# Last stage of a hybrid attention and MoE layer: the expert-row adds of six blocks on GpSimd, stores from the sync engine, one output buffer a block

## The chip, the cores and the metric

The kernel runs on one core of one Trainium2 chip. The metric is the device time of one execution in microseconds; for the kernel before it is the median of three runs. Smaller is better. A profile of one further execution gives the rows below.

## The reference, cut to what matters

The reference is one layer: 16 meta tokens are put ahead of 1024 frames of 1024 channels; RMSNorm, a combined input projection, two attention branches (latent attention, and sparse attention over 256 selected keys), gates, an output projection and a residual; then RMSNorm and a mixture of experts in which each token goes to two experts. The change touches only the end, which in the reference reads:

```python
out = jnp.zeros((N + 1, D), ys.dtype).at[slot_tok].add(ys * slot_w[:, None].astype(ys.dtype))
...
h = h + ffn.reshape(B, L, D_MODEL)
return rmsnorm(h, norm_final_g)[:, N_META:]
```

For each of the 1024 frames the two weighted expert rows are added, the sum is added to the residual `h`, and the row is normalised: divided by the root of its mean square plus 1e-6, times a gain for each channel. All of it is float32.

## The kernel before

The kernel is written for each engine by hand: every stage is a block in which each engine has its own list of instructions, and semaphores hold them together. An engine runs its list in order; a wait stops everything behind it on that engine. The stages are the norm and the projections, the attention branches, the gated output projection, the router tables, the loop over 32 experts (`experts`), a stage for experts with more than 128 rows (`overflow`), and the last stage, the function `final`. The experts leave their weighted rows in DRAM, in `ys_d`: 2048 rows of 4 KB, the first expert row of token t at t and the second at 1024 + t. The last stage starts when all of them are written.

`final` works on 8 blocks of 128 tokens (`NB` = 8, `P` = 128, `D` = 1024), one partition for each token. For block b:

- SyncE loads the two expert rows into `ya[b]` and `yb[b]` (tiles `fa` and `fb` in the trace), 512 KB each. All 16 loads, and the broadcast of the final gain into `gf`, are issued without any wait, since every block has buffers of its own. They go through the sync engine's queue.
- VectorE adds `yb[b]` to `ya[b]` (L2342), then adds that to the residual `h1[:, b, :]` (L2344, tile `h`).
- ScalarE squares the row and sums it (L2316, tile `fsq`, sum in `ss`).
- GpSimd makes the mean plus epsilon (L2325, `var`), then the power -0.5 (L2327, `rstd`), both on 128x1.
- VectorE multiplies the row by `rstd` and the gain into an output buffer (`finish`, L2337, tile `fo`), one block behind its adds: its order is fa(0), h(0), fa(1), h(1), fo(0), fa(2), h(2), fo(1), and so on up to fa(7), h(7), fo(6), fo(7).
- ScalarE issues the store of `fo` behind the square of the next block (L2319). There are four output buffers, so `finish(b)` for b from 4 on waits for the store of block b - 4.

Of the kernel before, what the change touches and what calls it, by code (L numbers as in the profile page):

```python
# [14 lines left out]
ALU = mybir.AluOpType  # L15
ACT = mybir.ActivationFunctionType
AX = mybir.AxisListType
F32 = mybir.dt.float32
# [4 lines left out]
P = 128  # L23
D = 1024
# [4 lines left out]
NB = T // P  # L29
# [1856 lines left out]
def experts(nc, a, at, sem, block, ps, flat, con, h1, nhalf, tabs, xn2_d, ys_d, out, R_H, R_K, ss, var, rstd,  # L1886
# [26 lines left out]
    with block() as blk:  # L1913
# [185 lines left out]
        def _(dve):  # L2099
# [72 lines left out]
            with dve.Fori(0, (NE - 4) // 4) as r:  # L2172
# [6 lines left out]
    overflow(nc, a, at, sem, block, ps, ident, xs, ye, xsT, sg, hm, hmT, tk, dk, wk, wts,  # L2179
             tok_i, dst_i, slot_w, ov_e, xn2_d, ys_d)  # L2180
    final(nc, a, at, sem, block, h1, nhalf, ys_d, out, R_K, R_H, ss, var, rstd)


# [104 lines left out]
def final(nc, a, at, sem, block, h1, nhalf, ys_d, out, R_K, R_H, ss, var, rstd):  # L2288

    ya = [at(f"fa{b}", [P, D], F32, R_K + 8192 * b) for b in range(NB)]  # L2290
    yb = [at(f"fb{b}", [P, D], F32, R_K + 8192 * b + 4096) for b in range(NB)]
    gf = at("gfin", [P, D], F32, R_K + 65536)
    sq = at("fsq", [P, D], F32, R_K + 69632)
    fo = [at(f"fo{k}", [P, D], F32, R_K + 73728 + 4096 * k) for k in range(4)]
    s_g, s_a1, s_a2, s_sq, s_v, s_r, s_o = map(sem, ["f_g", "f_a1", "f_a2", "f_sq", "f_v", "f_r", "f_o"])
    s_ls = [sem(f"f_l{b}") for b in range(NB)]
    s_sts = [sem(f"f_st{k}") for k in range(4)]
    with block() as blk:  # L2298
        @blk.sync
        def _(sp):  # L2300
            for b in range(NB):
                for k, t in enumerate((ya, yb)):
                    sp.dma_start(t[b][:, :], ys_d[T * k + P * b:T * k + P * (b + 1), :]).then_inc(s_ls[b], 16)  # L2303
                if b == 0:
                    sp.dma_start(gf[:, :], a["norm_final_g"].unsqueeze(0).to_broadcast([P, D])).then_inc(s_g, 16)  # L2305
            for k in range(4):
                sp.wait_ge(s_sts[k], 16 * NB // 4)

        @blk.scalar
        def _(act):  # L2310
            for b in range(NB + 1):
                if b < NB:
                    act.wait_ge(s_a2, b + 1)
                    if b:
                        act.wait_ge(s_sq, b)
                    act.activation(sq[:, :], h1[:, b, :], ACT.Square, accum_out=ss[:, b:b + 1]).then_inc(s_sq, 1)  # L2316
                if b:
                    act.wait_ge(s_o, b)
                    act.dma_start(out[0, P * (b - 1):P * b, :], fo[(b - 1) % 4][:, :]).then_inc(s_sts[(b - 1) % 4], 16)  # L2319

        @blk.gpsimd
        def _(pool):
            for b in range(NB):
                pool.wait_ge(s_sq, b + 1)
                pool.tensor_scalar(var[:, b:b + 1], ss[:, b:b + 1], 1.0 / D, EPS, ALU.mult, ALU.add).then_inc(s_v, 1)  # L2325
                pool.wait_ge(s_v, b + 1)
                pool.tensor_tensor(rstd[:, b:b + 1], var[:, b:b + 1], nhalf[:, b:b + 1], ALU.pow).then_inc(s_r, 1)  # L2327

        @blk.vector
        def _(dve):  # L2330
            def finish(b):
                dve.wait_ge(s_r, b + 1)
                if b == 0:
                    dve.wait_ge(s_g, 16)
                if b >= 4:
                    dve.wait_ge(s_sts[b % 4], 16 * (b // 4))
                dve.scalar_tensor_tensor(fo[b % 4][:, :], h1[:, b, :], rstd[:, b:b + 1], gf[:, :], ALU.mult,  # L2337
                                         ALU.mult).then_inc(s_o, 1)

            for b in range(NB):  # L2340
                dve.wait_ge(s_ls[b], 32)
                dve.tensor_tensor(ya[b][:, :], ya[b][:, :], yb[b][:, :], ALU.add).then_inc(s_a1, 1)  # L2342
                dve.wait_ge(s_a1, b + 1)
                dve.tensor_tensor(h1[:, b, :], h1[:, b, :], ya[b][:, :], ALU.add).then_inc(s_a2, 1)  # L2344
                if b:
                    finish(b - 1)
            finish(NB - 1)
# [21 lines left out]
```

## Time and profile before

| what | value |
|---|---|
| median of 3 runs | 1633.92 us (1629.78 to 1636.15) |
| the profiled execution: its own time | 1635.34 us |
| its span in the trace | 1633.4 us |
| first DMA issue of the last stage | 1591.14 us from the span's start |
| busy over the whole span: PE, DVE, ACT, POOL | 1434.7, 1052.9, 650.6, 405.3 us |

The last stage is the last 42.3 us of the span, 2.6% of it. PE does nothing there, so the shares of the whole span say nothing about it; what counts is the order of the small instructions on DVE (VectorE), ACT (ScalarE), POOL (GpSimd) and of the DMAs. Every time below is in us from the start of the span, unless it is marked ns. An instruction's row in the trace begins when its engine takes it up; where it is held up after that, its own duration in the row is longer.

### The profile page before, as it was taken

The numbers are of one execution on the slowest core, as the hardware profiler recorded it, in microseconds if no ns is written. First come the engines' busy times: TensorE is split into PE (matmuls) and PEld (weight loads), VectorE is DVE, ScalarE is ACT, GpSimd is POOL, SyncE is SP. The second block draws the span as 40 slices with busy tenths as digits, with TensorE's granted clock in tenths as the row PEclk, the third lists the DMA queues.
The fourth block names the chain that finished last, engine by engine and source line by source line (L and its number), as shares of the span: only waits on it lengthen the run. The fifth ranks groups of instructions, "written<-read, shape, count | busy, mean of one in ns | idle before, by whom it ended". The sixth has DMA issues, their size and how long they took to land. (4 is left out here: it accounts for less than half of the span.)

```text
span 1633.4 us, 21404 instructions
## 1 busy us (share of the span) xinstructions
PE 1434.7 (88%) x7182; PEld 1108.7 (68%) x7191; DVE 1052.9 (64%) x2047; ACT 650.6 (40%) x1129; POOL 405.3 (25%) x406
## 2 busy tenths in 40 slices
PE   6996899999999898988889888999945999999960
PEld 3465688889895457777667666889944777777730
DVE  4158999999922466666676665443254777777737
ACT  3157212121211236666666654021103666666622
POOL 1000322221211105454434411410002233333213
PEclk9998899999999999999999998999966999999985
DMA  7450122332231000302323204423154899999808
GB/s 195 51 87 14 58 81 87 103 97 91 73 117 42 1 0 1 72 1 66 75 60 82 66 1 161 157 87 104 65 219 182 321 357 357 356 367 376 328 31 319
DMA packets 86604, 216.82 MB, mean 133 GB/s; under 512 B 23720, under 2 KB 46792, under 8 KB 74232
## 3 DMA queue, kind: packets, MB, share of 16 engines
q1 hardware_dynamic: 76152, 194.72, 36.4%
q0 software_dynamic: 9216, 16.80, 2.8%
q10 hardware_dynamic: 1152, 4.19, 0.6%
q8 instruction: 51, 0.84, 0.2%
q14 instruction: 33, 0.27, 0.1%
HBM read 187.75 MB, written 44.70 MB: 142 GB/s over the span
## 5 line engine op out<-in xcount | busy, mean ns | idle before, releaser
L1193 DVE TENSOR_TENSOR pL<-ps,pH 128x512 fp32r<-128x512 f32 (+3 forms) x224 | 127.0, 574 | 114.4 <-ACT pH L1130 113.6
L457 DVE TENSOR_SCALAR_CACHE_REDUCE mask<-score,cand 128x272 bf16<-128x272 f32 (+6 forms) x224 | 185.5, 892 | 5.0 <-DVE cand L476 4.9
L2102 DVE TENSOR_TENSOR w_rest<-wgu,w_lead 128x1024 fp32r<-128x1024 f32 x128 | 156.0, 1223 | 45.0 <-ACT w_lead L2049 43.8
L542 PE MATMUL ps<-hHi,g_lead 128*128 128x512 f32 (+2 forms) x416 | 158.6, 381 | 16.2 <-DVE hLo L582 16.2
L543 PE MATMUL ps<-hLo,g_lead 128*128 128x512 f32 (+2 forms) x416 | 158.8, 382 | 0.0
L544 PE MATMUL ps<-hHi,g_rest 128*128 128x512 f32 (+2 forms) x416 | 158.0, 380 | 0.0
L2049 ACT CAST w_lead<-wgu 128x1024 fp32r<-128x1024 f32 x128 | 134.4, 1055 | 37.9 <-PE ps L1995 37.9
L1130 ACT CAST pH<-ps 128x512 fp32r<-128x512 f32 (+3 forms) x224 | 107.7, 488 | 71.5 <-PE ps L1078 70.5
L1993 PE MATMUL ps<-w_lead,x_lead 128*128 128x512 f32 x256 | 114.2, 446 | 6.0 <-DVE w_rest L2102 6.0
L577 POOL TENSOR_TENSOR g_rest<-g_raw,g_lead 128x2048 fp32r<-128x2048 f32 x13 | 61.7, 4745 | 227.8 <-ACT g_lead L551 227.8
L2015 PE MATMUL ps<-wd,hmT 128*128 128x512 f32 x256 | 115.3, 593 | 1.6 <-DVE hmT L2125 1.0
L1995 PE MATMUL ps<-w_lead,x_rest 128*128 128x512 f32 x256 | 101.8, 397 | 0.0
L542 PEld LDWEIGHTS ps<-hHi,g_lead 128*128 128x128 f32 x416 | 79.0, 190 | 32.9 <-issue 11.2
L1994 PE MATMUL ps<-w_rest,x_lead 128*128 128x512 f32 x256 | 100.9, 394 | 0.0
L1094 PE MATMUL ps<-pH,VS 128*128 128x512 f32 (+3 forms) x224 | 98.5, 440 | 0.2
L544 PEld LDWEIGHTS ps<-hHi,g_rest 128*128 128x128 f32 x416 | 79.1, 190 | 13.9
L543 PEld LDWEIGHTS ps<-hLo,g_lead 128*128 128x128 f32 x416 | 78.9, 190 | 14.0
L1955 POOL DMA_INDIRECT ys_d<-ye,dk x32 | 32.5, 1015 | 213.7 <-DVE ye L2137 213.7
L1095 PE MATMUL ps<-pL,VS 128*128 128x512 f32 (+3 forms) x224 | 81.4, 363 | 0.0
L563 ACT ACTIVATE stage<-ps 128x512 f32<-128x512 f32 x32 | 19.2, 598 | 151.9 <-PE ps L544 151.9
L2015 PEld LDWEIGHTS ps<-wd,hmT 128*128 128x128 f32 x256 | 46.2, 190 | 47.8 <-issue 47.8
L356 PE MATMUL ps<-hT,wslot 128*128 128x512 f32 (+2 forms) x176 | 72.1, 573 | 2.3 <-DMA wslot<-in_w_in 2.3
(332 smaller groups left out, 3453.1 us busy)
## 6 DMA issues: line engine op xcount, KB each, us to landing
wgu<-in_w_exp_gate SPq DMA_DIRECT2D x32, 1024.0 KB
wgu<-in_w_exp_up SPq DMA_DIRECT2D x32, 1024.0 KB
wd<-in_w_exp_down SPq DMA_DIRECT2D x32, 1024.0 KB
g_raw<-in_w_in SPq DMA_DIRECT2D x14, 1024.0 KB, 5.5
gates_d<-stage SPq DMA_DIRECT2D x32, 256.0 KB, 2.0
gt<-gates_d SPq DMA_DIRECT2D x32, 256.0 KB, 3.2
rel_d<-relf SPq DMA_DIRECT2D x1, 4672.0 KB
KR<-kb_d SPq DMA_DIRECT2D x16, 260.0 KB, 6.0
```

The lines of the kernel that those rows point to most:

```text
L457: return dve.tensor_scalar(mask[:, OFF[i]:OFF[i + 1]], score[:, OFF[i]:OFF[i + 1]], thr, 0.0, op, ALU.add, accum_out=cnt[:, i:i + 1])
L542: pe.matmul(dst, x[0], y[0], start=(k == 0), stop=False)
L543: pe.matmul(dst, x[0], y[1], start=False, stop=False)
L544: mm = pe.matmul(dst, x[1], y[0], start=False, stop=(k == KT - 1))
L1130: act.copy(pH[n % RING][:, lo:512], bank_of(k)[:, lo:512]).then_inc(s_ld, 1)
L1193: dve.tensor_tensor(pL[n % RING][:, lo:512], bank_of(k)[:, lo:512], pH[n % RING][:, lo:512].bitcast(F32), ALU.subtract).then_inc(s_rs, 1)
L1993: pe.matmul(dst, xl[:, k, :], wl, start=(k == 0), stop=False)
L1994: pe.matmul(dst, xl[:, k, :], wr, start=False, stop=False)
L1995: mm = pe.matmul(dst, xr[:, k, :], wl, start=False, stop=(k == KT - 1))
L2015: mm = pe.matmul(ps[:, 5 + half, :], hmT[u % 2][:, k, :], wd[u][:, k, 512 * half:512 * (half + 1)], start=(k == 0), stop=(k == 1))
L2049: act.copy(w_lead[part][:, :, :, :], wgu[u][:, :, 2 * part:2 * part + 2, :]).then_inc(S["m_wl"], 1)
L2102: dve.tensor_tensor(w_rest[u][:, :, 2 * part:2 * part + 2, :], wgu[u][:, :, 2 * part:2 * part + 2, :], w_lead[part][:, :, :, :].bitcast(F3 ...
```

## The change

In `final`, the add of the two expert rows for blocks 1 to 6 is made by GpSimd, one block ahead of its `var` and `rstd`: its list becomes add(b + 1), var(b), rstd(b). VectorE keeps that add for blocks 0 and 7 and waits for GpSimd's in between. The stores are issued by SyncE behind all the loads, each once the loads of a block four later (or of the last) have landed and `fo` of its block is written; ScalarE issues none. There are eight output buffers in place of four, so `finish` waits for no store.

```diff
--- before.py
+++ after.py
@@ -2291,10 +2291,11 @@
     yb = [at(f"fb{b}", [P, D], F32, R_K + 8192 * b + 4096) for b in range(NB)]
     gf = at("gfin", [P, D], F32, R_K + 65536)
     sq = at("fsq", [P, D], F32, R_K + 69632)
-    fo = [at(f"fo{k}", [P, D], F32, R_K + 73728 + 4096 * k) for k in range(4)]
-    s_g, s_a1, s_a2, s_sq, s_v, s_r, s_o = map(sem, ["f_g", "f_a1", "f_a2", "f_sq", "f_v", "f_r", "f_o"])
+    fo = [at(f"fo{b}", [P, D], F32, R_K + 73728 + 4096 * b) for b in range(NB)]
+    s_g, s_ad, s_ap, s_h, s_sq, s_v, s_r, s_o, s_st = map(
+        sem, ["f_g", "f_ad", "f_ap", "f_h", "f_sq", "f_v", "f_r", "f_o", "f_st"])
     s_ls = [sem(f"f_l{b}") for b in range(NB)]
-    s_sts = [sem(f"f_st{k}") for k in range(4)]
+    on_pool = range(1, NB - 1)
     with block() as blk:
         @blk.sync
         def _(sp):
@@ -2303,24 +2304,26 @@
                     sp.dma_start(t[b][:, :], ys_d[T * k + P * b:T * k + P * (b + 1), :]).then_inc(s_ls[b], 16)
                 if b == 0:
                     sp.dma_start(gf[:, :], a["norm_final_g"].unsqueeze(0).to_broadcast([P, D])).then_inc(s_g, 16)
-            for k in range(4):
-                sp.wait_ge(s_sts[k], 16 * NB // 4)
+            for b in range(NB):
+                sp.wait_ge(s_ls[min(b + 4, NB - 1)], 32)
+                sp.wait_ge(s_o, b + 1)
+                sp.dma_start(out[0, P * b:P * (b + 1), :], fo[b][:, :]).then_inc(s_st, 16)
+            sp.wait_ge(s_st, 16 * NB)
 
         @blk.scalar
         def _(act):
-            for b in range(NB + 1):
-                if b < NB:
-                    act.wait_ge(s_a2, b + 1)
-                    if b:
-                        act.wait_ge(s_sq, b)
-                    act.activation(sq[:, :], h1[:, b, :], ACT.Square, accum_out=ss[:, b:b + 1]).then_inc(s_sq, 1)
+            for b in range(NB):
+                act.wait_ge(s_h, b + 1)
                 if b:
-                    act.wait_ge(s_o, b)
-                    act.dma_start(out[0, P * (b - 1):P * b, :], fo[(b - 1) % 4][:, :]).then_inc(s_sts[(b - 1) % 4], 16)
+                    act.wait_ge(s_sq, b)
+                act.activation(sq[:, :], h1[:, b, :], ACT.Square, accum_out=ss[:, b:b + 1]).then_inc(s_sq, 1)
 
         @blk.gpsimd
         def _(pool):
             for b in range(NB):
+                if b + 1 in on_pool:
+                    pool.wait_ge(s_ls[b + 1], 32)
+                    pool.tensor_tensor(ya[b + 1][:, :], ya[b + 1][:, :], yb[b + 1][:, :], ALU.add).then_inc(s_ap, 1)
                 pool.wait_ge(s_sq, b + 1)
                 pool.tensor_scalar(var[:, b:b + 1], ss[:, b:b + 1], 1.0 / D, EPS, ALU.mult, ALU.add).then_inc(s_v, 1)
                 pool.wait_ge(s_v, b + 1)
@@ -2329,19 +2332,22 @@
         @blk.vector
         def _(dve):
             def finish(b):
-                dve.wait_ge(s_r, b + 1)
                 if b == 0:
                     dve.wait_ge(s_g, 16)
-                if b >= 4:
-                    dve.wait_ge(s_sts[b % 4], 16 * (b // 4))
-                dve.scalar_tensor_tensor(fo[b % 4][:, :], h1[:, b, :], rstd[:, b:b + 1], gf[:, :], ALU.mult,
+                dve.wait_ge(s_r, b + 1)
+                dve.scalar_tensor_tensor(fo[b][:, :], h1[:, b, :], rstd[:, b:b + 1], gf[:, :], ALU.mult,
                                          ALU.mult).then_inc(s_o, 1)
 
+            added = 0
             for b in range(NB):
-                dve.wait_ge(s_ls[b], 32)
-                dve.tensor_tensor(ya[b][:, :], ya[b][:, :], yb[b][:, :], ALU.add).then_inc(s_a1, 1)
-                dve.wait_ge(s_a1, b + 1)
-                dve.tensor_tensor(h1[:, b, :], h1[:, b, :], ya[b][:, :], ALU.add).then_inc(s_a2, 1)
+                if b in on_pool:
+                    dve.wait_ge(s_ap, b - on_pool[0] + 1)
+                else:
+                    dve.wait_ge(s_ls[b], 32)
+                    added += 1
+                    dve.tensor_tensor(ya[b][:, :], ya[b][:, :], yb[b][:, :], ALU.add).then_inc(s_ad, 1)
+                    dve.wait_ge(s_ad, added)
+                dve.tensor_tensor(h1[:, b, :], h1[:, b, :], ya[b][:, :], ALU.add).then_inc(s_h, 1)
                 if b:
                     finish(b - 1)
             finish(NB - 1)
```

VectorE, from the start of the stage. The numbers behind tile names tell buffers apart: `fa_14653` is `ya[1]`, `fb_14661` is `yb[1]`, `fo_14670` is the first output buffer. The kernel before:

```order
L2342 TENSOR_TENSOR fa_14652<-fa_14652,fb_14660 128x1024
L2344 TENSOR_TENSOR h_10538<-h_10538,fa_14652 128x1024
L2342 TENSOR_TENSOR fa_14653<-fa_14653,fb_14661 128x1024
L2344 TENSOR_TENSOR h_10538<-h_10538,fa_14653 128x1024
L2337 SCALAR_TENSOR_TENSOR fo_14670<-h_10538,rstd,gfin 128x1024
L2342 TENSOR_TENSOR fa_14654<-fa_14654,fb_14662 128x1024
L2344 TENSOR_TENSOR h_10538<-h_10538,fa_14654 128x1024
L2337 SCALAR_TENSOR_TENSOR fo_14671<-h_10538,rstd,gfin 128x1024
```

The same place in the changed kernel:

```order
L2348 TENSOR_TENSOR fa_14652<-fa_14652,fb_14660 128x1024
L2350 TENSOR_TENSOR h_10538<-h_10538,fa_14652 128x1024
L2350 TENSOR_TENSOR h_10538<-h_10538,fa_14653 128x1024
L2338 SCALAR_TENSOR_TENSOR fo_14670<-h_10538,rstd,gfin 128x1024
L2350 TENSOR_TENSOR h_10538<-h_10538,fa_14654 128x1024
L2338 SCALAR_TENSOR_TENSOR fo_14671<-h_10538,rstd,gfin 128x1024
```

The adds of `fa` are gone from VectorE for blocks 1 to 6; the order of what is left is the same.

GpSimd, from its first instruction of the stage, in the changed kernel (before, the stage's list held only the pairs of `var` and `rstd`):

```order
L2326 TENSOR_TENSOR fa_14653<-fa_14653,fb_14661 128x1024
L2328 TENSOR_SCALAR var<-ss 128x1
L2330 TENSOR_TENSOR rstd<-var,nhalf 128x1
L2326 TENSOR_TENSOR fa_14654<-fa_14654,fb_14662 128x1024
L2328 TENSOR_SCALAR var<-ss 128x1
L2330 TENSOR_TENSOR rstd<-var,nhalf 128x1
```

The add of block 1 now stands ahead of the `var` and `rstd` of block 0, the add of block 2 ahead of those of block 1, up to block 6.

## Rows read from the trace of the kernel before

**Rows 1.** The chain that ended last: start, duration, what.

```profile
1593.04 8.18 DMA fb<-ys_d
...
1601.24 1.24 DVE fa L2342
...
1628.98 1.28 DVE fo L2337
```

**Rows 2.** Timeline, first blocks: start, duration, engine, line, operation, idle before.

```profile
1599.65 0.19 POOL L2325 TENSOR_SCALAR var<-ss 128x1 f32<-128x1 f32 x1 [18.35 <-ACT fsq L2316]
...
1599.92 0.57 POOL L2327 TENSOR_TENSOR rstd<-var,nhalf 128x1 f32<-128x1 f32 x1
...
1600.85 1.06 SPq L2303 DMA_DIRECT2D fb<-ys_d  x1
...
1604.84 1.22 DVE L2342 TENSOR_TENSOR fa<-fa,fb 128x1024 f32<-128x1024 f32 x1
...
1604.99 1.11 POOL L2325 TENSOR_SCALAR var<-ss 128x1 f32<-128x1 f32 x1 [4.49 <-ACT fsq L2316]
1606.09 1.23 DVE L2344 TENSOR_TENSOR h<-h,fa 128x1024 f32<-128x1024 f32 x1
1606.18 1.53 POOL L2327 TENSOR_TENSOR rstd<-var,nhalf 128x1 f32<-128x1 f32 x1
...
1607.75 1.28 DVE L2337 SCALAR_TENSOR_TENSOR fo<-h,rstd,gfin 128x1024 f32<-128x1024 f32 x1 [0.44 <-POOL rstd L2327]
...
1608.58 0.50 POOL L2325 TENSOR_SCALAR var<-ss 128x1 f32<-128x1 f32 x1 [0.86 <-ACT fsq L2316]
1608.95 1.22 DVE L2342 TENSOR_TENSOR fa<-fa,fb 128x1024 f32<-128x1024 f32 x1
...
1609.17 1.41 POOL L2327 TENSOR_TENSOR rstd<-var,nhalf 128x1 f32<-128x1 f32 x1
```

**Rows 3.** Timeline, last blocks.

```profile
1616.67 1.22 DVE L2342 TENSOR_TENSOR fa<-fa,fb 128x1024 f32<-128x1024 f32 x1
...
1623.18 1.28 DVE L2337 SCALAR_TENSOR_TENSOR fo<-h,rstd,gfin 128x1024 f32<-128x1024 f32 x1 [0.44 <-POOL rstd L2327]
...
1625.63 1.23 DVE L2344 TENSOR_TENSOR h<-h,fa 128x1024 f32<-128x1024 f32 x1
```

**Rows 4.** Windows of the stage: engines' busy us (count), clock, DMA share, GB/s.

```profile
1610.00:1615.00 5.00, 0.00 (x0) 0.00 (x0) 4.93 (x5) 1.15 (x2) 2.79 (x3) 0.50 1.03 420
...
1620.00:1625.00 5.00, 0.00 (x0) 0.00 (x0) 4.53 (x5) 1.48 (x4) 3.56 (x4) 0.50 0.29 119
```

**Rows 5.** GpSimd groups of the whole span: operation, shapes, count, busy us, mean ns.

```profile
L1259 POOL TENSOR_TENSOR KL<-KTa,KH 96x1040 fp32r<-96x1040 f32 x7 | 17.0, 2422 | 0.6
L1240 POOL TENSOR_TENSOR q_rest<-QTa,q_lead 96x1024 fp32r<-96x1024 f32 x7 | 16.6, 2377 | 0.6
```

**Rows 6.** Timeline of GpSimd and of VectorE, 1019 to 1024 us.

```profile
1019.58 1.29 POOL L1584 TENSOR_TENSOR yT<-ytmp 128x512 f32<-128x512 f32 x1 [7.02 <-DVE ytmp L1517]
1022.14 2.13 POOL L1584 TENSOR_TENSOR yT<-ytmp 128x512 f32<-128x512 f32 x1 [1.28 <-DVE ytmp L1517]
...
1021.91 1.22 DVE L1499 TENSOR_TENSOR wb_rest<-wbr,wb_lead 128x1024 fp32r<-128x1024 f32 x1
```

**Rows 7.** Line L582, both engines: duration ns min/median/max, first and last start.

```profile
L582 POOL TENSOR_TENSOR hLo<-hT,hHi x4: 2572/3394/3401, 160.3 to 169.5; 128x1040 fp32r<-128x1040 f32 x4
L582 DVE TENSOR_TENSOR hLo<-hT,hHi x4: 3426/3430/3442, 160.5 to 170.6; 128x1040 fp32r<-128x1040 f32 x4
```

**Rows 8.** GpSimd's first two of these in its timeline.

```profile
160.28 2.57 POOL L582 TENSOR_TENSOR hLo<-hT,hHi 128x1040 fp32r<-128x1040 f32 x1 [135.64 <-ACT hHi L555]
...
162.82 3.40 POOL L582 TENSOR_TENSOR hLo<-hT,hHi 128x1040 fp32r<-128x1040 f32 x1
```

**Rows 9.** The stage's stores: ns of an issue on ScalarE's queue, min/median/max.

```profile
L2319 ACTq DMA_DIRECT2D out<-fo x8: 338/338/395, 1605.0 to 1630.3; - x8
```

## The prediction

> **What bounds the stage now.** I read the chain that ended last first, because the change lies in the last 42 us and only what ends last there can move the time. The chain waits for the loads of block 1 until 1601.22 [rows 1]; from there it never leaves the loop VectorE, ScalarE, GpSimd, VectorE. The timeline of the stage shows what that loop costs: VectorE's add of block 2 starts at 1604.84 and that of block 5 at 1616.67 [rows 2, 3], three blocks in 11.83 us, so 3.94 a block early on. Its own work in a block is fa 1.22, h 1.23 and fo 1.28, which overlap by some hundredths. So VectorE is nearly full, as the windows say too (4.5 to 4.9 us busy in 5) [rows 4]. The DMA engines are at 1.03 of their time from 1610 to 1615 and at 0.29 from 1620 to 1625 [rows 4], so the transfers are nearly through while the loop still has 10 us to go. The last fo begins at 1628.98 and ends at 1630.26 [rows 1]; the last store is some 3.1 us more, to the end of the span at 1633.4.
>
> On its face, then, the change takes a third of the work off the engine that bounds. The second thing to read is what GpSimd's tiny instructions do beside VectorE. Alone, var takes 0.19 and rstd 0.57 [rows 2]. Beside VectorE, var takes 1.11 (1604.99 to 1606.10, and VectorE's fa ends at 1606.06) and rstd 1.53 (1606.18 to 1607.71, and h ends at 1607.32). The next rstd ends 0.41 after VectorE's fa. So a GpSimd instruction that reads SBUF is held until VectorE's instruction with two SBUF inputs ends, and then finishes 0.04 (var) or 0.40 (rstd) later. It holds beside fo as well: var of 1608.58 ends at 1609.08, and fo at 1609.03 [rows 2]. It also slips in there between two VectorE instructions that follow each other.
>
> **What a GpSimd add costs, alone and beside VectorE.** The trace has no GpSimd add of this very shape, but near ones: 2.38 us for 1024 columns, 2.42 for 1040 [rows 5], and 1.29 for 512 columns of plain float32 on 128 partitions [rows 6], which is the same rate. I take 2.38. Held up by VectorE, the 512-column add took 2.13: VectorE's instruction ended at 1023.13, the add at 1024.27, 1.14 later, so it has 0.15 of its 1.29 behind it while it waits [rows 6]. A held add of 1024 columns then ends 2.23 after VectorE's.
>
> The other direction is at 160 to 174 us, where both engines made two-input subtractions of 1040 columns, four each. GpSimd's took 3.39 to 3.40 and VectorE's 3.43 [rows 7], where one alone is 2.42 and about 1.25. GpSimd's first two end at 162.85 and 166.22 [rows 8], 3.37 apart: 2.27 of GpSimd and 1.10 of VectorE, strictly one after the other. So VectorE is held as fully as GpSimd, and comes out 1.10 after the add ends; I take 1.09 for 1024 columns.
>
> The Trainium skill has this as a rule ("SBUF — State Buffer", section "Who interferes with whom"): a VectorE instruction with two SBUF inputs and a GpSimd instruction that reads SBUF exclude each other, and the second one blocks until the first is done. The trace agrees in both directions, with the overlap of about 0.15 that the rows give. By the rule taken literally, with full durations in turn, the result is the heavy rival below; by the rows it is the sum that follows.
>
> **The change, part by part.** *The adds.* All of VectorE's instructions here (fa, h, fo) have two SBUF inputs, and so has GpSimd's add. What was 1.2 us of VectorE becomes 2.2 to 2.4 us in which VectorE can't work either. Start: block 1 lands at 1601.21 as before (the loads ahead of it are the same); GpSimd adds from 1601.24 to 1603.62. Which of two goes first afterwards, the next add or the waiting fo, the trace doesn't tell (they become ready within some 0.05 us), so I work out both.
>
> (A) The add goes first. From the end of one add: held fo(b-1) 1.09, h(b+1) directly behind it 1.23 - 0.08 = 1.15 (fo to fa starts are 1.20 apart at a duration of 1.28 [rows 2]), var slips in, rstd 0.40 after h, the next add 2.38: 5.02 a block. The first round has no fo: 0.03 + 1.23 + 0.40 + 2.38 = 4.04. The add of block 6 ends at 1603.62 + 4.04 + 4 x 5.02 = 1627.74. Then fo(4) 1.09, h(6) 1.15, rstd(5) 0.40, 0.02 to start fo(5); from the start of fo(5) to the end of h(7) as before (1623.18 to 1626.86 [rows 3]: 3.68); and from there to the end of fo(7) as before (to 1630.26: 3.40). Last fo ends at 1637.48: 7.2 later.
>
> (B) fo goes first. A round is 0.03 + 1.23 (h), 0.40 (rstd), 0.02 + 1.28 (fo), 2.23 (held add): 5.19. Block 6's add ends at 1603.62 + 5 x 5.19 = 1629.57, and 1.26 + 0.40 + 0.02 + 3.68 + 3.40 = 8.76 more gives 1638.33: 8.1 later.
>
> The two bound the orders; I take the middle, +7.6.
>
> *var and rstd behind the add.* rstd(0) is late by the whole add of block 1; that is in the rounds above. Behind it on GpSimd waits only the next add.
>
> *Loads.* They are ahead all the time: at the 420 GB/s of [rows 4] a block's 1.05 MB takes 2.5, so block b lands at about 1601.2 + 2.5 (b - 1) with no store between, block 6 at 1613.7, and its add is not due before 1625.
>
> *Stores.* The last store alone is on the path. Its issue is 0.34 on ScalarE's queue [rows 9]; one of SyncE's issues took 1.06 at 1600.85, with many transfers queued [rows 2], and at the end there are next to none. I take +0.1, between 0 and 0.7. The stores that queue behind loads wait for nobody, with eight buffers. All loads are issued by 1601.9 [rows 2], so no store stands ahead of one. In the kernel before fo(5) waits for rstd, not for its buffer's store [rows 3], so four more buffers free nothing. ScalarE loses eight issues in its idle time: nothing.
>
> *Sum:* +7.7 on the profiled execution's own 1635.34, so 1643.0 for a profiled one; the profiled run is 1.4 above the median 1633.92, and against the median it gives 1641.6.
>
> **Rivals.**
> - *No exclusion for this add* (the GpSimd add reads beside VectorE). GpSimd would need 2.38 + 0.19 + 0.57 and 0.15 of gaps, 3.3 a block; block 6's add at 1603.62 + 16.5 = 1620.1, the last fo at 1620.1 + 1.26 + 0.02 + 3.68 + 3.40 = 1628.5, 1.8 earlier: 1632.1. For it speaks only that GpSimd is idle enough; against it the eight instructions of line L582 [rows 7]. It decides if the adds take 2.4 in the stage while VectorE's rows stay at 1.2. Even with no cost on GpSimd at all, block 7 lands at 1616.2 and needs fa and h 2.49 and the tail 3.40: 1622.1, a gain of 8.2. A gain over 0.5% (8.2 us) is therefore out of reach.
> - *Heavy handing over.* Each of the five instructions of a round costs its full own duration in turn: 1.28 + 1.23 + 0.19 + 0.57 + 2.38 and 0.15 of gaps, 5.8. Block 6's add at 1603.62 + 29.0 = 1632.6, the last fo 8.8 later at 1641.4: +11.1, so 1645.0. For it: VectorE now hands over three times in a round. Against it: each handing over in the rows was cheaper than that.
> - *VectorE keeps the port for two instructions in a row and GpSimd waits for both,* or the other way round. In (A) and (B) VectorE never has more than two to give; one more wait of 0.4 a block gives +9.7, so 1643.6.
>
> **How the numbers follow.** The serial sum between 7.2 and 8.1 (1641 to 1642 against the median): 0.75. Heavy handing over or the extra wait: 0.17. No exclusion: 0.05; the rest is something unseen. The three runs of before spread by 6 us, so a median of a few runs is good to about 2 us; a difference can be told from none at about 0.5%, which is 8.2 us. My sum ends right under that bound, 0.47%. Below it fall a bit over half of the serial case and the no-exclusion case, above it the rest and the heavy cases: same 0.50, slower 0.46, faster 0.04. The range 1636.8 to 1645.8 leaves out no exclusion and the far end of the heavy case.
>
> **What would show it.** In the profile after: GpSimd's adds of about 4.5 to 4.7 where held by fo and h, or 2.4 where VectorE waits; VectorE's h or fo beside them with rows of 2.5 to 3.5 or idle time put down to GpSimd's `fa`; about 5.0 to 5.2 us from one h to the next for blocks 2 to 6, against 3.9 before; the last fo near 1638; DMA share falling to near zero well before the end; and in the chain that ended last, GpSimd's add with 10 us or more in place of VectorE's. The prediction is wrong if h to h is under 4 (then there is no exclusion) or over 5.5 (then handing over costs more), or if the last store lands more than 4 us after the last fo.

## The result, and the profile after

Over all runs the changed kernel takes 1638.96 us (median of 15, 1635.75 to 1643.21) and the kernel before 1631.02 us (median of 15, 1626.76 to 1636.19). The ratio is 1.0047, 95% interval 1.0034 to 1.0060: 7.7 us slower, 5.5 to 9.8. The forecast was +7.7 us and 1641.6 us in a range of 1636.8 to 1645.8. It was added to the median of three runs of the kernel before, 1633.92.

The two profiled spans, 1633.4 and 1636.1 us, are only 2.7 apart. The reason lies ahead of the change: the last stage begins at 1591.14 in the one and at 1587.17 in the other, and in the eight experiments between 1582.25 and 1590.87, though nothing ahead of it differs. So the stage itself is compared, from its first DMA issue: 42.26 us before (to 1633.4), 48.93 after (to 1636.1). Within it the cleanest stretch is from the moment block 1 is ready (the start of its add) to the end of the last fo: 29.02 us before, 36.12 after, a difference of 7.10. Below, this is called the stretch, and a round is the time from the start of one h to the start of the next.

The chain that ended last, in the changed kernel: start, duration, what. One round in the middle and the tail:

```profile
1589.12 7.73 DMA fb<-ys_d
...
1596.92 2.33 POOL fa L2326
...
1606.17 2.31 POOL fa L2326
1608.48 0.08 issue
1608.57 1.06 POOL var L2328
1609.62 0.07 issue
1609.70 1.41 POOL rstd L2330
1611.11 2.31 POOL fa L2326
...
1625.95 1.28 DVE fo L2338
1627.23 1.15 DVE fa L2348
```

From block 1 to block 6 the chain now goes through GpSimd alone: add, var, rstd, add. Of the 4.94 us of a round only 2.31 is the add; the 1.06 and 1.41 belong to two instructions that need 0.19 and 0.55 to 0.57 alone. Where that time goes is seen in the timeline of the same round (compare [rows 2]):

```profile
1606.14 2.34 POOL L2326 TENSOR_TENSOR fa<-fa,fb 128x1024 f32<-128x1024 f32 x1
1606.20 3.36 DVE L2338 SCALAR_TENSOR_TENSOR fo<-h,rstd,gfin 128x1024 f32<-128x1024 f32 x1 [0.44 <-POOL rstd L2330]
...
1608.57 1.05 POOL L2328 TENSOR_SCALAR var<-ss 128x1 f32<-128x1 f32 x1
1609.49 1.21 DVE L2350 TENSOR_TENSOR h<-h,fa 128x1024 f32<-128x1024 f32 x1
1609.70 1.41 POOL L2330 TENSOR_TENSOR rstd<-var,nhalf 128x1 f32<-128x1 f32 x1
...
1611.08 2.34 POOL L2326 TENSOR_TENSOR fa<-fa,fb 128x1024 f32<-128x1024 f32 x1
1611.14 3.36 DVE L2338 SCALAR_TENSOR_TENSOR fo<-h,rstd,gfin 128x1024 f32<-128x1024 f32 x1 [0.44 <-POOL rstd L2330]
```

VectorE's fo starts 0.06 us behind GpSimd's add and stays in its row for 3.36 us, 1.08 of them after the add has ended (1608.48 to 1609.56). Then var is done 0.06 after fo, h runs until 1610.70, and rstd is done 0.41 after h. Apart from a tenth or two at each change from one engine to the other, no two of the five do their work side by side. The six adds read alike, none of them held. Of the eight fo, the five beside an add take 3.28 to 3.36 us, and the three with no add beside them 1.28. The views of the two lines (duration in ns, min/median/max):

```profile
L2326 POOL TENSOR_TENSOR fa<-fa,fb x6: 2333/2337/2342, 1596.9 to 1621.0; 128x1024 f32<-128x1024 f32 x6
```

```profile
L2338 DVE SCALAR_TENSOR_TENSOR fo<-h,rstd,gfin x8: 1278/3318/3364, 1601.3 to 1631.8; 128x1024 f32<-128x1024 f32 x8
```

A window shows how "busy" misleads here, against the same window in [rows 4]: both engines look nearly full, and the DMA engines are idle three quarters of the time.

```profile
1620.00:1625.00 5.00, 0.00 (x0) 0.00 (x0) 4.56 (x3) 1.15 (x2) 4.83 (x4) 0.50 0.26 105
```

VectorE is shown busy for 4.56 of 5 us with three instructions in the window; in the kernel before it was 4.53 us with five.

### The profile page after: what moved, and what is told of

Its sections match the earlier page's. It is cut to its first block and busy times, and to the rows that moved or that the text cites. A ratio compares the mean times of both kernels' runs of the same rounds, so it can differ in the third digit from the quotient of the medians.

```text
span 1636.1 us, 21406 instructions
## 1 busy us (share of the span) xinstructions
PE 1432.5 (88%) x7182; PEld 1107.0 (68%) x7191; DVE 1056.0 (65%) x2041; ACT 650.8 (40%) x1129; POOL 422.1 (26%) x412
## 5 line engine op out<-in xcount | busy, mean ns | idle before, releaser
L1213 POOL TENSOR_TENSOR otok<-otmp,rec 128x256 f32<-128x256 f32 x32 | 19.7, 614 | 214.7 <-DVE otmp L1200 214.7
```

## The experiments

All were compared with the kernel before on the same chip. The stretch is read from the profiled execution, one for each kernel.

| kernel | stretch, us | against 29.02 | ratio to before, 95% interval |
|---|---|---|---|
| the change | 36.12 | +7.10 | 1.0047 (1.0034 to 1.0060) |
| adds_only | 36.10 | +7.08 | 1.0031 (1.0017 to 1.0045) |
| stores_only | 29.01 | -0.01 | 0.9998 (0.9986 to 1.0011) |
| gain_psum | 32.69 | +3.67 | 1.0023 (1.0011 to 1.0034) |
| both_psum | 26.77 | -2.25 | 0.9989 (0.9976 to 1.0002) |
| three_adds | 32.02 | +3.00 | 1.0018 (1.0009 to 1.0028) |
| no_adds_psum | 27.39 | -1.63 | 0.9989 (0.9976 to 1.0002) |
| three_adds_psum | 25.65 | -3.37 | 0.9984 (0.9972 to 0.9996) |
| three_late_psum | 25.54 | -3.48 | 0.9990 (0.9978 to 1.0001) |

The theory is that VectorE's instructions with two SBUF inputs and GpSimd's that read SBUF exclude each other, so that an add moved to GpSimd takes 2.2 us from VectorE in place of 1.2. The rivals are the stores' new place, a loss from GpSimd's latency or list whatever it reads, and a cost that is paid once and not for each add.

### Half of the change each: adds_only and stores_only

adds_only takes the changed kernel and puts the stores back as they were, with four output buffers (cut to the store itself):

```diff
-                sp.dma_start(out[0, P * b:P * (b + 1), :], fo[b][:, :]).then_inc(s_st, 16)
...
+                    act.dma_start(out[0, P * (b - 1):P * b, :], fo[(b - 1) % 4][:, :]).then_inc(s_sts[(b - 1) % 4], 16)
```

> The six adds go to GpSimd as in the change; the stores stay on ScalarE's queue with four output buffers, as before. If the cost is the port that VectorE and GpSimd exclude each other from, the whole loss is here: a round of 4.94 us between the starts of h for blocks 2 to 6, as in the changed kernel, the last fo some 36.1 us after block 1 is ready (29.0 before), and a ratio to before of 1.004 to 1.005. If the loss (or a part of it) came from the stores behind the loads on SyncE's queue, the round is shorter and the ratio nearer 1.

stores_only keeps the stores and puts the adds back on VectorE:

```diff
-    on_pool = range(1, NB - 1)
+    on_pool = []
```

> SyncE issues the stores behind the loads, with eight output buffers; all adds stay on VectorE. If the port is the cause: a round of 3.86 us as before, 29.0 us from block 1 ready to the last fo, 3.1 us from there to the end, ratio 1.000 (within 0.15%). If the stores' place costs or gains: more or less than 3.1 us at the end, or waits of fo.

adds_only repeats the changed kernel's stretch to 0.02 us, stores_only that of before to 0.01. From the end of the last fo to the end of the span it is 3.14 us before, 3.06 in the changed kernel, 3.10 and 3.11 in these two. The ratio of adds_only, 1.0031, is lower than the expected 1.004 to 1.005, but its interval holds the 1.0043 that 7.1 us would make. So the loss is in the adds, and the stores' queue and the four more buffers cost or bring nothing that these runs can show.

### Taking the exclusion away and leaving the adds: gain_psum and both_psum

gain_psum reads the final gain from PSUM (`flat` is the PSUM tile), where ScalarE copies it once (1.02 us, while it waits for loads); `finish(0)` waits for that copy in place of the load:

```diff
+    gp = flat[:, 0:D]
...
+            act.wait_ge(s_g, 16)
+            act.copy(gp, gf[:, :]).then_inc(s_gp, 1)
...
-                dve.scalar_tensor_tensor(fo[b][:, :], h1[:, b, :], rstd[:, b:b + 1], gf[:, :], ALU.mult,
+                dve.scalar_tensor_tensor(fo[b][:, :], h1[:, b, :], rstd[:, b:b + 1], gp, ALU.mult,
```

> The changed kernel, with the final gain copied once to PSUM by ScalarE, so that VectorE's fo has one SBUF input in place of two; everything else as in the changed kernel. If two SBUF inputs are what excludes GpSimd: fo falls from 3.36 us in its row to about 1.3 and lies beside the add of 2.33; a round is h 1.26, var 0.11 behind it, rstd 0.57, add 2.33, about 4.3 us in place of 4.94, and the stage some 3.5 us shorter than the changed kernel's (ratio to before about 1.002 to 1.003). If VectorE is held by a GpSimd instruction whatever it reads: fo stays at 3.3 and the round at 4.94, ratio 1.0047.

Timeline of gain_psum, one round:

```profile
1609.42 2.35 POOL L2330 TENSOR_TENSOR fa<-fa,fb 128x1024 f32<-128x1024 f32 x1
1609.49 1.28 DVE L2342 SCALAR_TENSOR_TENSOR fo<-h,rstd,ps 128x1024 f32<-128x1024 f32 x1 [0.71 <-POOL rstd L2334]
...
1611.80 1.22 DVE L2354 TENSOR_TENSOR h<-h,fa 128x1024 f32<-128x1024 f32 x1 [1.03 <-POOL fa L2330]
1611.85 1.22 POOL L2332 TENSOR_SCALAR var<-ss 128x1 f32<-128x1 f32 x1
...
1613.15 0.55 POOL L2334 TENSOR_TENSOR rstd<-var,nhalf 128x1 f32<-128x1 f32 x1
```

The same fo starts 0.07 us behind the same add, and takes 1.28 where it took 3.36. Nothing else was changed on VectorE or GpSimd, so it is the gain read from SBUF, fo's second input there, that let the add hold it. The round is 4.25 (h starts at 1607.55 and 1611.80), as worked out. What still has two SBUF inputs, h, still holds var: 1.22 in place of 0.19.

both_psum does the same for h. ScalarE copies each block's residual to PSUM ahead of its add, three slots in turn:

```diff
+                if b + 3 < NB:
+                    act.copy(hp(b + 3), h1[:, b + 3, :]).then_inc(s_hp, 1)
...
-                dve.tensor_tensor(h1[:, b, :], h1[:, b, :], ya[b][:, :], ALU.add).then_inc(s_h, 1)
+                dve.wait_ge(s_hp, b + 1)
+                dve.tensor_tensor(h1[:, b, :], hp(b), ya[b][:, :], ALU.add).then_inc(s_h, 1)
```

> As the one before, and ScalarE also copies each block of the residual to PSUM ahead of h's add (three slots in turn), so that neither h nor fo has two SBUF inputs. With the port theory nothing but the fa of blocks 0 and 7 excludes GpSimd any more: var 0.19, rstd 0.57, add 2.33 and gaps 0.2 to 0.3 make a round of about 3.3 us, bound by GpSimd; the last fo comes about 27 us after block 1 is ready, 2 us sooner than before; ratio about 0.999. If ScalarE's extra copies (about 1.1 us a block beside the square of 1.25) or slower reads of PSUM bind, the round is longer than 3.3; if the exclusion has another cause, it stays above 4.9.

Timeline of both_psum, one round:

```profile
1610.09 1.23 DVE L2364 TENSOR_TENSOR h<-ps,fa 128x1024 f32<-128x1024 f32 x1 [0.82 <-POOL fa L2339]
1610.14 0.19 POOL L2341 TENSOR_SCALAR var<-ss 128x1 f32<-128x1 f32 x1
1610.42 0.55 POOL L2343 TENSOR_TENSOR rstd<-var,nhalf 128x1 f32<-128x1 f32 x1
1610.93 2.35 POOL L2339 TENSOR_TENSOR fa<-fa,fb 128x1024 f32<-128x1024 f32 x1
1611.23 1.27 DVE L2351 SCALAR_TENSOR_TENSOR fo<-h,rstd,ps 128x1024 f32<-128x1024 f32 x1
```

Now every row of the round has the duration that it has alone, within 0.02 us, var 0.19 and rstd 0.55 among them, and the round is 3.23 us, GpSimd's own list from end to end. VectorE waits 0.82 for each add. The only long row left is a var of 1.10 us at 1622.28, beside VectorE's add of block 7, which still reads two tiles from SBUF. The kernel with the six adds, 7.10 us behind the kernel before with the exclusion, is 2.25 ahead of it without: this is the prediction's first rival, made true (its round was 3.3 us and its gain 1.8). How much of the 2.25 the moved adds bring is measured below. The ratio, 0.9989, can't be told from 1.

Here the Trainium skill ("SBUF — State Buffer", section "Who interferes with whom") says that a VectorE instruction with at most one SBUF input, outside the modes that use both ports, does not contend with GpSimd. The rows of both kernels agree (fo 1.28 beside the add in gain_psum, var 0.19 beside h in both_psum).

### Half the dose: three_adds

```diff
-    on_pool = range(1, NB - 1)
+    on_pool = [2, 4, 6]
```

> The changed kernel with GpSimd's adds for blocks 2, 4 and 6 only; VectorE makes the other five. All from SBUF. If each moved add costs the difference of the two engines' exclusive time (2.2 of GpSimd for 1.2 of VectorE), two blocks take about 8.7 us where before took 7.7 and the changed kernel 9.9; the last fo comes some 32 us after block 1 is ready (29.0 before, 36.1 changed), ratio about 1.002. If a cost of another kind (the first wait on GpSimd, the order on its list) made the loss, three adds cost as much as six, 36 us.

Timeline of three_adds, one moved add with what holds it and what it holds:

```profile
1610.08 1.41 POOL L2330 TENSOR_TENSOR rstd<-var,nhalf 128x1 f32<-128x1 f32 x1
1611.12 1.22 DVE L2350 TENSOR_TENSOR h<-h,fa 128x1024 f32<-128x1024 f32 x1
1611.46 3.08 POOL L2326 TENSOR_TENSOR fa<-fa,fb 128x1024 f32<-128x1024 f32 x1
1612.26 3.37 DVE L2338 SCALAR_TENSOR_TENSOR fo<-h,rstd,gfin 128x1024 f32<-128x1024 f32 x1
```

Three adds cost 3.00 us in the stretch, 1.00 for each, where six cost 7.10, 1.18 for each. Two blocks take 8.54 (h at 1607.01 and 1615.55), against 8.7 expected. Here both directions are seen at once: the add waits for h, which ends at 1612.34, and comes 2.20 later at 1614.54; fo waits for the add and comes 1.09 after it. A loss that is only paid once is excluded.

### Is it PSUM that gains? no_adds_psum

The kernel both_psum with `on_pool = []`: all adds on VectorE.

> No add on GpSimd; the gain and the residual are read from PSUM, so that h and fo have one SBUF input each; stores as in the changed kernel. With the port theory rstd is held by fa alone, the waits of 0.44 us in every second block go, and the round falls from 3.86 to about 3.6 us: the last fo 27.2 to 27.5 us after block 1 is ready, ratio 0.999. If PSUM inputs in themselves changed VectorE's pace, its rows of 1.22 to 1.28 would change; if they did nothing, 29.0.

```profile
1607.84 1.23 DVE L2364 TENSOR_TENSOR h<-ps,fa 128x1024 f32<-128x1024 f32 x1
1607.94 0.55 POOL L2343 TENSOR_TENSOR rstd<-var,nhalf 128x1 f32<-128x1 f32 x1
1608.98 1.27 DVE L2351 SCALAR_TENSOR_TENSOR fo<-h,rstd,ps 128x1024 f32<-128x1024 f32 x1
1610.17 1.22 DVE L2361 TENSOR_TENSOR fa<-fa,fb 128x1024 f32<-128x1024 f32 x1
```

VectorE's rows are as long as before (1.22 to 1.27), and the round is 3.58 in place of alternately 3.59 and 4.12: rstd, beside h, takes 0.55 and not 1.53 and is no longer late. The kernel before itself lost 1.6 us to the exclusion: three of its rounds had the wait of 0.44 that [rows 2, 3] show in front of fo, and each of them was 0.53 longer than the others. So PSUM alone brings 1.63 of both_psum's 2.25, and six adds on GpSimd only 0.6 more: with six, GpSimd's list of 3.23 us a round binds.

### Three adds without the exclusion: three_adds_psum and three_late_psum

three_adds_psum is both_psum with `on_pool = [3, 5, 7]`.

> Gain and residual from PSUM, GpSimd's adds for blocks 3, 5 and 7. Nothing but VectorE's own fa excludes GpSimd. VectorE is left with 21 instructions of about 1.2 us in place of 24; GpSimd's add, behind its rstd, comes about 0.6 us late in every second block. The last fo 25 to 26 us after block 1 is ready, 3 to 4 sooner than before; ratio 0.9975 to 0.9985. Rival: the loads, which need 15 us from block 1 to block 7, or GpSimd's latency bind, and it is no better than 27.

```profile
1606.20 1.22 DVE L2361 TENSOR_TENSOR fa<-fa,fb 128x1024 f32<-128x1024 f32 x1
1606.37 1.10 POOL L2341 TENSOR_SCALAR var<-ss 128x1 f32<-128x1 f32 x1 [1.62 <-ACT fsq L2330]
...
1607.55 0.55 POOL L2343 TENSOR_TENSOR rstd<-var,nhalf 128x1 f32<-128x1 f32 x1
1608.07 2.36 POOL L2339 TENSOR_TENSOR fa<-fa,fb 128x1024 f32<-128x1024 f32 x1
1608.59 1.27 DVE L2351 SCALAR_TENSOR_TENSOR fo<-h,rstd,ps 128x1024 f32<-128x1024 f32 x1
...
1610.45 1.23 DVE L2364 TENSOR_TENSOR h<-ps,fa 128x1024 f32<-128x1024 f32 x1 [0.59 <-POOL fa L2339]
```

25.65 us, 3.37 below before, and a ratio of 0.9984 whose interval (0.9972 to 0.9996) ends just below 1 and holds the 0.9979 that 3.37 us would make: of all versions, this is the only one whose timed runs show it ahead of the kernel before. The wait of 0.6 in front of h in every second block is the one that the expectation named. The rows above say more of it. The add stands behind var and rstd, and this var is held by VectorE's fa, the one kind of instruction with two SBUF inputs that is left: 1.10 us in place of 0.19. An estimate from these rows: with a var of 0.19 the add would end 0.9 sooner, and the wait of 0.6 would be gone. No run tests that.

three_late_psum adds one edit to it:

```diff
-                if b:
-                    finish(b - 1)
-            finish(NB - 1)
+                if b >= 2:
+                    finish(b - 2)
+            finish(NB - 2)
+            finish(NB - 1)
```

> As the one before, and VectorE's fo comes two blocks behind h in place of one, so that neither a late rstd nor the last square holds it. VectorE should run without a gap from block 3 on: 24 to 25 us from block 1 ready to the last fo, ratio 0.997. If it isn't below three_adds_psum by 0.5 us or more in that stretch, the latency of rstd was not what was left.

This was a miss. The stretch is 25.54, only 0.11 shorter. The last fo no longer waits 0.94 for its rstd, but h of block 3 now waits 1.31 in place of 0.60, since one fo less stands ahead of it and the add waits for its loads (0.59 on GpSimd). Outside the stretch 0.9 is lost again: the last stores are issued closer together, and the span ends 4.01 us after the last fo instead of 3.13. The ratios of the two versions can't be told apart. The later blocks still wait 0.6 for the add, so fo's wait for rstd was not what cost them that. What did is the add's place on GpSimd's list, behind a var that fa holds here too (1.10 us at 1610.20, beside fa at 1610.04):

```profile
1607.71 1.23 DVE L2364 TENSOR_TENSOR h<-ps,fa 128x1024 f32<-128x1024 f32 x1 [1.31 <-POOL fa L2339]
...
1614.29 1.22 DVE L2364 TENSOR_TENSOR h<-ps,fa 128x1024 f32<-128x1024 f32 x1 [0.59 <-POOL fa L2339]
```

Neither another order on that list (the add ahead of the var and rstd of two blocks back) nor an fa with one input in PSUM was tried, so how the 0.6 divides between the two stays open. That the last stores compete is read from one profile and not tested.

## Why the prediction was right

**What bounds.** Right: VectorE's list with its short waits for rstd. What the prediction did not say is that these waits were already the exclusion's; no_adds_psum put 1.63 us on them.

**The price of a held instruction.** Right in each part. Of the round of case (A) 5.02 was forecast and 4.94 measured: held fo 1.09 against 1.08 after the add's end, h 1.15 against 1.14, rstd 0.40 against 0.41, the add 2.38 against 2.31 (an add of plain float32 is 2.33 to 2.34 and overlaps rstd's row by 0.03). The prices of the add and of the held fo came from other stages of the same trace and carried over within 0.07; so did that of a held add, 2.23 for case (B), which three_adds measured at 2.20. Two readings on the way were loose. The 512-column add is not quite "the same rate" (1.29 us is 2.5 ns a column, 2.38 for 1024 is 2.3), and not all four of GpSimd's subtractions took 3.39 to 3.40: the first took 2.57 [rows 7, 8]. The sum rests on neither.

**Which goes first.** Left open between (A) and (B); it was (A) in every round. The add's row starts 0.06 before fo's (0.13 the first time), and fo is the one held. After the first add it is the other way round: h starts at 1599.29, var at 1599.35, and var is the one held. In all of these pairs the earlier start won.

**The first round.** 4.04 forecast, 4.29 measured from the end of the first add (1599.25) to the end of the second (1603.54). In (A) var was to slip in before h ends; with no fo ahead of h there is no place for it, so rstd began only after h and was done 0.70 after it, not 0.40.

**The sum.** 36.24 for case (A) from block 1's add to the last fo, 36.12 measured: the first round's excess and the cheaper adds cancel. The middle with (B) that I took was 0.5 too high, and the +0.1 for SyncE's stores was -0.1. The timed runs give +7.7 with about 2 us to each side, so only the traces can tell such tenths, and that the forecast was +7.7 to the tenth is luck: the traces make it about 7.0. The time itself was forecast 2.6 us too high (1641.6 against 1638.96), since the median of three runs to which it was added lies 2.9 above the 1631.02 of 15 runs. The prediction also held that a difference under 0.5% can't be told from none. With 15 runs each it can: the interval of the ratio starts at 1.0034.

**Loads and stores.** Right: the loads are never waited for after block 1, and stores_only measured the stores at nothing.

**Signs.** VectorE's fo beside the add had the row of 2.5 to 3.5 us that was forecast (3.36), the round of 4.94 us is 0.06 under the 5.0 to 5.2, GpSimd's six adds are 13.9 us of the chain, and the last store landed 3.06 after the last fo. No add took 4.5 to 4.7: each took 2.33 to 2.34, unheld, and the waiting was in the rows of var, rstd and fo. The DMA share fell to 0.26 and not to near zero.

**Rivals.** Heavy handing over and the extra wait are out: rounds of 4.94 and not 5.8 or 5.4. No exclusion is out for this kernel and was built in both_psum. The bound of 8.2 us on any gain was not approached: the most that a version won in the stretch is 3.5.

## What to carry to other kernels

Before an instruction is moved from VectorE to GpSimd, look for places in the trace where both engines worked at once: if tiny GpSimd instructions end a few hundredths after VectorE's big ones, the two don't run side by side, and the move costs GpSimd's longer time in place of VectorE's (here 1.0 to 1.2 us for each add). The "busy" share can't show it, since an instruction that is held counts as busy. If one input of VectorE's instructions can live in PSUM, the two can run side by side, as here; then count GpSimd's list first, for it becomes the bound soon (here six adds brought 0.6 us and three 1.7 beyond what PSUM alone gave), and look at what still reads two tiles from SBUF, since it still holds GpSimd (var 1.10 us beside fa).

## What the runs showed of the hardware that I had not expected

An input moved from SBUF to PSUM changed nothing in the duration of VectorE's instructions (fo 1.28 and 1.27, h 1.23) but freed GpSimd: rstd beside h took 0.55 in place of 1.41 to 1.53, and the add beside fo stayed at 2.33 to 2.36. ScalarE's copy of 128x1024 float32 to PSUM took 1.00 to 1.02 us, a price that its idle time hid.

Of two instructions that start within 0.13 us of each other, the earlier one went first in all the rows read here: five times the add before fo (0.13 us apart once, 0.06 four times), once h before var (0.06).
